# Sums of w_out's merged pairs made in the gates stage and loaded like weights, four merged pairs per half for three

## The reference, cut to what matters

```
proj = rms_norm(x, attn_norm_g) @ w_in            # q, k, v, index and gate columns
o_sb, o_ds = two attention branches, 8 heads each
merged = sigmoid(g_sb) * (o_sb @ w_branch[:SB_W]) + sigmoid(g_ds) * (o_ds @ w_branch[SB_W:])
x = x + merged @ w_out                            # w_out: 2048 x 2048
u = causal_depthwise_conv(rms_norm(x, ffn_norm_g) @ w_up, conv_w, conv_b)
gate, val = split(u)
x = x + (silu(gate) * val) @ w_down
```

## Time and profile before

| | us |
|---|---|
| median of three runs (1435.15 to 1435.22) | 1435.2 |
| the profiled execution | 1435.17 |
| its span in the trace | 1433.3 |
| PE busy, PEld busy | 1427.8, 1222.9 |
| DVE, ACT, POOL busy | 1138.3, 841.5, 448.0 |
| gates, from its second head on, per head | 25.7 |
| out, first to last product | 624.4 to 708.7 |

### The profile page before, as it was taken

One profiled execution on the slowest core, in us unless ns is written; L12 is line 12 of the kernel. 1 busy time (PEld: TensorE's weight loads), 2 busy tenths in 40 slices (PEclk: granted clock), 3 DMA queues, 4 the chain that ended last, 5 costly groups with the idle time before them and its releaser, 6 DMA issues.

```text
span 1433.3 us, 23700 instructions
## 1 busy us (share of the span) xinstructions
PE 1427.8 (100%) x7626; PEld 1222.9 (85%) x7626; DVE 1138.3 (79%) x1503; ACT 841.5 (59%) x1181; POOL 448.0 (31%) x493
## 2 busy tenths in 40 slices
PE   9999999999999999999999999999999999999999
PEld 7888888888888888888888888888888888888887
DVE  6778998886656566899967778777778778999998
ACT  7545667666767666666664455455554545465553
POOL 2310000333132213650025455655556555200000
PEclk9999999999999999999999999999999999999999
DMA  8565665655554545567555565566665565566664
GB/s 260 187 197 172 209 195 186 193 176 176 161 162 160 167 170 178 189 221 234 192 178 184 183 202 181 186 191 190 190 191 185 180 198 185 192 232 206 204 207 148
DMA packets 121063, 272.25 MB, mean 190 GB/s; under 512 B 10688, under 2 KB 10976, under 8 KB 121008
## 3 DMA queue, kind: packets, MB, share of 16 engines
q1 hardware_dynamic: 119936, 268.99, 58.1%
q0 software_dynamic: 896, 2.42, 0.6%
q10 hardware_dynamic: 176, 0.14, 0.0%
HBM read 269.42 MB, written 2.10 MB: 189 GB/s over the span
## 4 chain that ended last, share of the span: by engine, by line
PE 99%; DMA 0%; DVE 0%; DVEq 0%; issue 0%
PE bank L2098 98%; PE bank L2152 1%; DMA y<-in_x 0%; PE bank L2371 0%; PE bank L2412 0%; DVE y L1770 0%; PE bank L2235 0%; PE bank L2171 0%; PE bank L2213 0%; DVE y L1815 0%; DVEq L201 0%; PE bank L2220 0%; PE bank L2210 0%; PE bank L2202 0%; DVEq L529 0%
## 5 line engine op out<-in xcount | busy, mean ns | idle before, releaser
L1100 DVE TENSOR_TENSOR lo<-raw,hi 128x1024 fp32r<-128x1024 f32 (+1 forms) x342 | 444.3, 1304 | 167.0 <-ACT hi L639 166.3
L639 ACT ACTIVATE hi<-raw 128x1024 fp32r<-128x1024 f32 (+1 forms) x342 | 359.2, 1053 | 271.6 <-PE bank L2098 266.9
L2098 PE MATMUL bank<-h2T,hi 128*128 128x512 f32 x1408 | 483.3, 394 | 0.0
L2098 PE MATMUL bank<-h2T,lo 128*128 128x256 f32 x1408 | 376.8, 278 | 0.0
L2098 PEld LDWEIGHTS bank<-h2T,hi 128*128 128x128 f32 x1408 | 257.9, 188 | 53.5
L2098 PE MATMUL bank<-hT,hi 128*128 128x512 f32 (+1 forms) x784 | 272.9, 395 | 0.0
L2098 PEld LDWEIGHTS bank<-h2T,lo 128*128 128x128 f32 x1408 | 264.4, 188 | 7.8
L2098 PE MATMUL bank<-hT,lo 128*128 128x256 f32 (+1 forms) x784 | 212.6, 281 | 0.0
L2062 POOL TENSOR_TENSOR u<-u,rms_row 128x256 f32<-128x256 f32 x88 | 120.9, 1374 | 184.7 <-DVE u L1621 165.7
L2098 PE MATMUL bank<-hi,ffT 128*128 128x512 f32 x576 | 177.4, 389 | 0.0
L2098 PEld LDWEIGHTS bank<-hT,hi 128*128 128x128 f32 (+1 forms) x784 | 143.9, 187 | 29.4
(11 more groups left out here) (292 smaller groups left out, 2017.6 us busy)
## 6 DMA issues: line engine op xcount, KB each, us to landing
raw<-in_w_up SPq DMA_DIRECT2D x176, 512.0 KB, 3.5
raw<-in_w_in SPq DMA_DIRECT2D x160, 512.0 KB, 3.4
raw<-in_w_down SPq DMA_DIRECT2D x88, 512.0 KB, 4.4
raw<-in_w_branch SPq DMA_DIRECT2D x32, 512.0 KB, 3.6
raw<-in_w_out SPq DMA_DIRECT2D x24, 512.0 KB, 4.6
raw4h<-in_w_in SPq DMA_DIRECT2D x8, 512.0 KB, 3.4
raw5h<-in_w_in SPq DMA_DIRECT2D x8, 512.0 KB, 4.4
raw45m<-in_w_out SPq DMA_DIRECT2D x8, 512.0 KB, 4.9
```

Source lines behind the costliest of these rows:

```text
L639: act.activation(hi[s][:, 0:width], raw[s][:, 0:width], ACT.Copy)\
L1100: dve.tensor_tensor(lo[s][:, 0:width], raw[s][:, 0:width], hi[s][:, 0:width].bitcast(f32), ALU.subtract)\
L2098: return pe.matmul(o, l, r, start=start, stop=stop, skip_group_check=True)
```

## The change

The weight sums of w_out's merged pairs leave DVE's program in out and branch. In the gates stage, once per head, SP loads one pair's tiles into a buffer `out_pre` (in the order B1, right half of B2, left half of B2), DVE adds them in place in three adds after its sixth, seventh and eighth chunk, SP stores the 1 MB to a DRAM tensor `out_sums`, and in out they are loaded like weight chunks, two loads of 512 KB per merged pair. `out_pre` is used again by the next head, so SP waits for the store before the next three loads. With eight heads there are eight such pairs: four merged pairs per half (0 to 3) where there were three. The first tile of a merged pair is loaded with its 512 columns alone, since nothing else reads the rest. A half has 24 chunks now and the stage 48 loads. The steps that are counted from the last merged pair keep their counts.

```
-    OUT_SUMMED = 3
+    OUT_SUMMED = 4
-    OUT_ORDER = [[("plain", 4)] + turns(0, 5, 1, 6, 2, 3) + [("plain", 7)],
-                 turns(0, 4, 1, 5, 2, 6) + [("plain", 3), ("plain", 7)]]
+    OUT_ORDER = [[("plain", 4), ("summed", 0), ("summed", 1), ("plain", 5), ("summed", 2), ("summed", 3),
+                  ("plain", 6), ("plain", 7)],
+                 [("summed", 0), ("plain", 4), ("summed", 1), ("plain", 5), ("summed", 2),
+                  ("summed", 3), ("plain", 6), ("plain", 7)]]
...
-    ROW_S = [s for s in ROW_STEPS + OUT_STEPS if s.made is not None]
+    ROW_S = [s for s in ROW_STEPS if s.made is not None]
...
+        out_pre = at("out_pre", [4 * GRP], 48 * KB)
+        out_sums = nc.dram_tensor("out_sums", (2 * OUT_SUMMED * P, 4 * GRP), f32,
+                                  kind="Internal").ap()
...
             def load_step(step, w, col):
-                for k in range(2):
+                for k in range(4 if step.stored else 2):
...
+                    width = GRP if step.stored and k == 0 else BLOCK
+                    if k < 2:
+                        kt = 2 * step.pair + k
+                        src = w[kt * P:(kt + 1) * P, ds(col, width)]
+                    else:
+                        row = (2 * step.pair + step.m - NB) * P
+                        src = out_sums[row:row + P, (k - 2) * BLOCK:(k - 1) * BLOCK]
+                    load(slot, raw_s[stage(step)][slot][:, 0:width], src)
...
+            def out_turn(pair, m):
+                i = 2 * pair + m
+                row, col = 2 * P * pair, m * BLOCK
+                def before(j):
+                    if j == 0:
+                        wait_alone(sp, out_stored, 16 * i + 1)
+                        sp.dma_start(out_pre[:, 0:2 * GRP], w_out[ds(row, P), col:col + BLOCK])\
+                            .then_inc(out_landed, 16)
+                        sp.dma_start(out_pre[:, 2 * GRP:3 * GRP],
+                                     w_out[ds(row + P, P), col + GRP:col + BLOCK])\
+                            .then_inc(out_landed, 16)
+                        sp.dma_start(out_pre[:, 3 * GRP:4 * GRP],
+                                     w_out[ds(row + P, P), col:col + GRP])\
+                            .then_inc(out_landed, 16)
+                    if j == 6:
+                        wait_alone(sp, out_summed, 3 * i + 3)
+                        sp.dma_start(out_sums[ds(P * i, P), :], out_pre[:, :])\
+                            .then_inc(out_stored, 16)
+                return before
...
-            with sp.Fori(0, 8) as g:
-                load_group(C_GATES, w_in, CPG * g, GATE_AT + GRP * g)
+            load_group(C_GATES, w_in, 0, GATE_AT)
+            with sp.Fori(0, OUT_SUMMED - 1) as q:
+                for m in range(2):
+                    load_group(C_GATES, w_in, CPG * (2 * q + m + 1), GATE_AT + GRP * (2 * q + m + 1),
+                               before=out_turn(q, m))
+            load_group(C_GATES, w_in, CPG * 7, GATE_AT + GRP * 7, before=out_turn(OUT_SUMMED - 1, 0))
+            load_group(C_BRANCH, w_branch, 0, 0, before=out_turn(OUT_SUMMED - 1, 1))
+            wait_alone(sp, out_stored, 16 * 2 * OUT_SUMMED + 1)
...
+                    if j == 5:                      # gates_body of DVE
+                        dve.wait_ge(out_landed, 48 * h + 48)
+                        dve.tensor_tensor(out_pre[:, 0:2 * GRP], out_pre[:, 0:2 * GRP],
+                                          out_pre[:, GRP:3 * GRP], ALU.add).then_inc(out_summed, 1)
+                    if j == 6:
+                        dve.wait_ge(out_summed, 3 * h + 1)
+                        dve.tensor_tensor(out_pre[:, 2 * GRP:3 * GRP], out_pre[:, 0:GRP],
+                                          out_pre[:, 2 * GRP:3 * GRP], ALU.add)\
+                            .then_inc(out_summed, 1)
+                    if j == 7:
+                        dve.wait_ge(out_summed, 3 * h + 2)
+                        dve.tensor_tensor(out_pre[:, 3 * GRP:4 * GRP], out_pre[:, 2 * GRP:3 * GRP],
+                                          out_pre[:, 3 * GRP:4 * GRP], ALU.add)\
+                            .then_inc(out_summed, 1)
...
-                    weight_sums(c)                  # branch_body and the loop of out
-            def out_sums(m, n):
+            def out_far(m, n):
```

More of the change, by code:

```diff
@@ L69, in hybrid_layer @@
     C_ROWS = KT // TAIL_CK
-    Step = namedtuple("Step", "m pair made chunk raw")
+    Step = namedtuple("Step", "m pair made chunk raw stored", defaults=(False,))
     S_BLOCKS = range(2, NB)
@@ L93, in block_steps @@
                 made = pair if kind == "summed" else None
-                table.append(Step(b, pair, made, chunk, raw + 2 * len(table)))
+                table.append(Step(b, pair, made, chunk, raw, stored and made is not None))
                 chunk += 2 if made is None else 4
+                raw += 4 if table[-1].stored else 2
             assert chunk == BLOCK_END[b]
@@ L537, in load, with load_group @@
                 sp.dma_start(dst, src).then_inc(w_landed[slot], 16)
-            def load_group(c0, w, step, col, n=CPG, width=GRP, per=CK):
+            def load_group(c0, w, step, col, n=CPG, width=GRP, per=CK, before=None):
                 for j in range(n):
+                    if before is not None:
+                        before(j)
                     wait_alone(sp, lo_done, c0 + j - AHEAD + step)
@@ L568, in load_step @@
                     if old is not None:
-                        was = (ROW_STEPS + OUT_STEPS)[old // 2]
-                        wait_alone(sp, lo_done, was.chunk + old % 2 + 1)
-                        if was.made is not None:
-                            wait_alone(sp, (sum13_done, sum4_done)[old % 2],
-                                       ROW_S.index(was) + 1)
+                        was, part_ = ROW_LOADED[old]
+                        wait_alone(sp, lo_done, was.chunk + part_ + 1)
+                        if was in ROW_S:
+                            wait_alone(sp, (sum13_done, sum4_done)[part_], ROW_S.index(was) + 1)
                     elif slot < SLOTS:
@@ L577, in load_step @@
                         wait_alone(sp, sig_done, 8 * 4)
-                    kt = 2 * step.pair + k
-                    load(slot, raw_s[stage(step)][slot][:, :],
-                         w[kt * P:(kt + 1) * P, ds(col, BLOCK)])
+                    width = GRP if step.stored and k == 0 else BLOCK
[6 more added lines that the diff above has]
+                    load(slot, raw_s[stage(step)][slot][:, 0:width], src)
             for step in ROW_STEPS:
@@ L708, in chunk_hi @@
                 (step, k), s = PART[c], c % SLOTS
-                if step.made is None or k < 2:
+                if step.made is None or step.stored or k < 2:
                     q = step.raw + k
@@ L713, in chunk_hi @@
                 elif k == 2:
-                    src = ssum13[stage(step)]
+                    src = hsum13
                     act.wait_ge(sum13_done, ROW_S.index(step) + 1)
                 else:
-                    src = ssum24[stage(step)]
+                    src = hsum24
                     act.wait_ge(sum2_done, ROW_S.index(step) + 1)
@@ L1210, in chunk_lo @@
                 (step, k), s = PART[c], c % SLOTS
-                if step.made is None or k < 2:
+                if step.made is None or step.stored or k < 2:
                     src = raw_s[stage(step)][ROW_SLOT[step.raw + k]]
                 else:
-                    src = (ssum13, ssum24)[k - 2][stage(step)]
+                    src = (hsum13, hsum24)[k - 2]
                 width = GRP if step.made is not None and k == 0 else 2 * GRP
@@ L1223, in weight_sums @@
                 for n, step in enumerate(ROW_S):
-                    first_at = step.chunk - (1 if stage(step) else 2)
-                    second_at = step.chunk + (1 if stage(step) and step.made == 1
-                                              else 0 if stage(step) else -1)
-                    b1, b2 = [raw_s[stage(step)][ROW_SLOT[step.raw + k]] for k in range(2)]
-                    s13, s24 = ssum13[stage(step)], ssum24[stage(step)]
-                    if c == first_at:
+                    b1, b2 = [raw_s[0][ROW_SLOT[step.raw + k]] for k in range(2)]
+                    s13, s24 = hsum13, hsum24
+                    if c == step.chunk - 2:
                         for q in (step.raw, step.raw + 1):
@@ L1233, in weight_sums @@
                             dve.wait_ge(lo_done, ROW_S[n - 1].chunk + 3)
-                        dve.wait_ge(left_done, 2 * stage(step) + 2)
+                        dve.wait_ge(left_done, 2)
                         slot = ROW_SLOT[step.raw]
-                        if slot < SLOTS or stage(step):
-                            both = (raw_two + [raw45m])[slot // 2]
+                        if slot < SLOTS:
+                            both = raw_two[slot // 2]
                             dve.tensor_tensor(s13[:, :].rearrange("p (n c) -> p n c", n=2),
```

(2 more changed lines are left out.)

32 lines of the change are left out of this document (18 added, 14 removed).

## The result

| kernel | median us | runs | lowest to highest | ratio to before (95%) |
|---|---|---|---|---|
| before | 1435.30 | 7 | 1435.15 to 1436.85 | |
| after | 1439.86 | 7 | 1438.14 to 1441.53 | 1.0031 (1.0020 to 1.0043) |

What follows compares the result with a forecast made beforehand. TensorE was taken to bound the kernel, with VectorE the near rival. Terms of -1.36 (two products), -0.55 (old waits), +2.0 (half 2) and +2.0 (entry of up) gave +2.1, so 1435.2 became 1437.3 us; range 1434.0 to 1440.8.

Steps and rivals of the forecast that it cites:

- gates stage: Eight heads, each with three more loads, three adds and a store: all hidden, price 0, at most 5 us.
- entry of up: Start of the up stage: TensorE waits 0.4 us for a transposed tile and 1.5 for a near add, sum 2.0.
- the likeliest case: The forecast itself, 1437.3 us, own range 1436.1 to 1438.4, chance 0.45.
- rival (a): Output stage: the load ring is short of bytes, +1 to +4 us on the sum, 1440.3 us; chance 0.27.
- before's waits for lo: Output stage of the kernel before: two TensorE waits for VectorE's remainders go, gaining 0.55 us.
- half 1: First half of the output stage: sums arrive as loads, VectorE no longer limits; 0 to 0.3 us, value 0.
- half 2, chunks 17 to 20: Output stage: TensorE waits for remainders delayed by near adds and ACT, 0.35, 1.0, 0.45 and 0.2, sum 2.0 us.
- t = 0: Moment in half 2 when chunk 15's step begins, put at 686.72 us, from which the chain of waits was timed.
- loads 18 and 19: Half 2's weight loads for chunks 18 and 19: landing in 6.6 us instead of 4.6 raises the loss bound to 3.2.
- (b): Rival for half 2 and the up stage's start: only one of the two stalls comes, 1435.3 us; chance 0.14.
- (c): Rival for half 2 and the up stage's start: neither stall comes, whole gain, 1433.3 us; chance 0.12.
- (d): Rival in the gates stage: stores or third add delay eight heads by 0.5 us each, 1441.3 us; chance 0.02.

Runs made afterwards that it cites:

- e10_bytes: e9_joins with each sum's load halved to 512 columns and read twice (output not the reference's): 1434.92 us.
- e6_three: Changed kernel with all eight sums made and stored, but three pairs per half merged, in the order before: 1434.91 us.
- e9_joins: Changed kernel, half 2's last merged pair two chunks earlier, landing tiles five and six used to chunk 17, near adds and half 1's far joins moved: 1436.78 us.
- e11_tiles: e9_joins with eight landing tiles in the output stage instead of six, nothing left out: 1434.14 us.
- e1_near: Changed kernel with VectorE's near adds and half 1's last far joins moved earlier in half 2: 1438.89 us.
- e5_direct: Changed kernel without the gates stage's loads, adds and stores; output stage loads unsummed w_out pieces of equal size (output not the reference's): 1438.14 us.

## Why the prediction was right, and where it was thin

The bound, the direction and the places were right: TensorE is the limit, six matmuls fewer, no cost in gates, waits for lo at chunks 17 to 20 of half 2, two waits at the entry of up. 1439.86 lies within 1434.0 to 1440.8, and outside the likeliest case's own range, 1436.1 to 1438.4. That the stated range holds it is in part luck: it reached so high for rival (a), whose 1440.3 us is the nearest number, by 2.2 us of missing bytes in each half that no profile shows, and 1.5 us of the measured 4.6 lie at the start and the end, where the prediction had nothing. Term by term, from the profiles, with the waits as their brackets give them:

| term | predicted | measured |
|---|---|---|
| two products | -1.36 | 7620 matmuls; -1.35 in e10_bytes' out stage |
| before's waits for lo | -0.55 | both gone; worth 0.27 (below) |
| gates stage | 0 | 0 (181.6 us in both) |
| half 1 | 0 | +0.32 |
| half 2, chunks 17 to 20 | 0.35 + 1.0 + 0.45 + 0.2 = 2.0 | 0.40 + 1.10 + 1.07 + 0.33 = 2.90 |
| entry of up | 0.4 + 1.5 = 2.0 | 0.65 + 1.69 = 2.34 |
| sum | +2.1 | +3.7 by the brackets, +2.9 by the stages |
| start, and behind the last product | not in it | +1.1, +0.4 |

Of the 0.8 us between the two sums, nearly all comes from reading the brackets as losses. After a wait the next product follows sooner than the usual 0.68 us. So the loss is read from the starts of products on both sides. In the changed kernel, around the four waits of half 2:

```profile
691.81 0.41 PEld L2152 LDWEIGHTS bank<-hi,mT 128*128 128x128 f32 x2
...
699.62 0.42 PEld L2152 LDWEIGHTS bank<-hi,mT 128*128 128x128 f32 x2
```

Eight products lie between, 5.44 us by the pace, and 7.81 have passed: a loss of 2.37, where the brackets add up to 2.90. The two waits of before, in the same way:

```profile
633.96 0.42 PEld L2098 LDWEIGHTS bank<-hi,mT 128*128 128x128 f32 x2
...
635.54 0.42 PEld L2098 LDWEIGHTS bank<-hi,mT 128*128 128x128 f32 x2
...
641.68 0.41 PEld L2098 LDWEIGHTS bank<-hi,left_m 128*128 128x128 f32 x2
...
643.09 0.42 PEld L2098 LDWEIGHTS bank<-hi,left_m 128*128 128x128 f32 x2
```

Each time two products, 1.36 us, took 1.58 and 1.41: the two waits cost 0.27 us and not 0.55, and e6_three, which has none, has an out stage 0.3 us shorter. The wait in half 1 cost 0.17 us (654.85 to 656.38 for two products), and the entry of up 0.61 and 1.50, its rows set against the same rows of before. With these, -1.36 - 0.27 + 0.17 + 2.37 + 2.1 = +3.0 us, against +2.9 by the stages. So the terms of the prediction were off by 0.3 us in before's waits, 0.4 in half 2, 0.2 in half 1 and 0.1 at the entry of up.

The mechanism of the named terms held, TensorE's loss to within 0.1 us at chunks 17 and 18 (0.26 and 0.97 us by the starts). The prediction took t = 0 from the row at 691.48, as the start of chunk 16; that is the chunk's second row, the first stands at 690.80. It did no harm, since a chunk's lo is first waited for in its second row. The sizes that were off are chunk 19, before's waits, half 1 and the two that no term held. Chunk 19 is the telling one (0.94 us by the starts, for 0.45): "loads 18 and 19" stood in my bounds only ("3.2, if [they] land in the longest 6.6 us"), as a matter of luck. They are late by construction. The table of landing tiles goes from six to four for the last loads. Before, these were four, all of plain chunks; with 48 loads for 32 they are eight, and begin at chunk 16 of half 2, the last merged pair. Load 19 is issued when the remainder of chunk 15 is done, at 689.86, and lands at 695.12, 5.3 us later. The prediction counted the change's loads and not their lead. So its rival (a) was half true and misnamed: the ring is near its limit in half 1 (0.94), but what TensorE waits for in half 2 is a load issued too late, and in the order of e9_joins eight tiles heal that with the same bytes (e11_tiles). In half 1 the bytes may still cost e11_tiles its four waits. Rival (a) put no price on it in half 2's last merged pair, where it mattered.

Of the two causes I named for half 2, removing the one (e1_near) gave 0.8 us of out, not the 2.9 of its brackets: two limits lay within a microsecond of each other, and the profile can only show the later. (b) and (c) are refuted, since both stalls are there, and (d) too, by the heads' 25.73 us. The 0.4 us behind the last product is in nearly all four-pair kernels (4.7 to 4.9 us from ffT's last weight loads to the end of the span, 4.4 in before, e5_direct and e6_three); its cause was not looked for.

## What to carry to other kernels

A sum made earlier and loaded like a weight trades VectorE's time for bytes and for lead: count for each load how many chunks ahead it is issued and how long these chunks last on TensorE, above all where a ring of buffers changes its length. When two engines' work has filled the same gap, take both away before you judge either; one edit alone shows only the other cause. A wait's length in brackets is not what it costs: read that from the starts of the work on both sides. And where the engine behind a wait is full, reordering within the full stretch moves the wait, so move the work that fills it (here the last merged pair) to another place.
